# Attention products on stacked high and low halves, in a ring of two head pairs

## The reference

```python
n = rms_norm(h, norm1_g[layer]);  proj = n @ w_in[layer]
mq = rms_norm(mq, moba_q_norm_g);  mk = rms_norm(mk, moba_k_norm_g)
p = softmax(mq @ mk.T * 64**-0.5 + t5_bias[bucket(distance)], causal)
y_moba = p @ mv
```

```python
c = cumsum(log_sigmoid(x @ w_f + b_f))
p = softmax(q @ k.T * 64**-0.5 + c[query] - c[key], causal)
y_fox = p @ v
```

## Time and profile before

| what | value |
|---|---|
| runs | 2238.19 us median, 2237.45 to 2238.38 |
| the profiled execution | 2238.22 us, of which the span is 2236.3 |
| outside the span | 1.9 us |
| PE busy | 2166.0 us, 97% of the span |
| DVE / ACT / POOL busy | 1072.5 / 840.2 / 124.7 us |
| mean granted TensorE clock | 0.986 |

### The profile page before, as it was taken

The page is one execution under the profiler, slowest core; times in us unless marked ns, Lnnn a source line. Parts: engine busy times, 40 slices in busy tenths (PEclk is TensorE's granted clock), DMA queues, the critical chain, the costliest instruction groups (busy, mean ns, idle before and its releaser), DMA issues.

```text
span 2236.3 us, 23914 instructions
## 1 busy us (share of the span) xinstructions
PE 2166.0 (97%) x9656; PEld 1691.4 (76%) x9656; DVE 1072.5 (48%) x1677; ACT 840.2 (38%) x1333; POOL 124.7 (6%) x121
## 2 busy tenths in 40 slices
PE   7999999999999999999998999998999998999997
PEld 5766767888888888766677888887766677888886
DVE  4443454655443444355466333337455466333336
ACT  4333232524332323333456243343433345342343
POOL 0000000000000000022001000002022002000001
PEclk9999999999999999999998999999999998999998
DMA  6211212422222322321222322231322221322221
GB/s 226 75 57 57 63 58 68 132 94 95 94 95 94 110 89 85 118 81 61 71 76 63 107 94 94 95 96 55 119 72 69 71 76 57 112 96 94 95 94 57
DMA packets 178794, 196.65 MB, mean 88 GB/s; under 512 B 6587, under 2 KB 164539, under 8 KB 178684
## 3 DMA queue, kind: packets, MB, share of 16 engines
q1 hardware_dynamic: 177120, 189.97, 26.6%
q0 software_dynamic: 1056, 4.72, 0.6%
q10 hardware_dynamic: 508, 0.43, 0.1%
HBM read 190.36 MB, written 4.75 MB: 87 GB/s over the span
## 4 chain that ended last, share of the span: by engine, by line
PE 90%; DVE 6%; ACT 3%; issue 1%; DMA 0%; ACTq 0%; DVEq 0%
PE ps L251 24%; PE ps L254 24%; PE ps L253 24%; PE ps L524 3%; PE ps L561 2%; PE ps L319 2%; PE ps L324 2%; PE ps L322 2%; PE ps L547 1%; PE ps L1291 1%; ACT H L1005 1%; PE ps L1277 1%; DVE wl L224 1%; ACT Phi L1008 1%; DVE d L952 1%
## 5 line engine op out<-in xcount | busy, mean ns | idle before, releaser
L251 PE MATMUL ps<-Phi,wh 128*128 128x512 f32 (+1 forms) x1520 | 614.3, 404 | 34.5 <-DVE Plo L1009 20.6
L254 PE MATMUL ps<-Phi,wl 128*128 128x512 f32 (+1 forms) x1520 | 588.7, 387 | 0.0
L253 PE MATMUL ps<-Plo,wh 128*128 128x512 f32 (+1 forms) x1520 | 588.4, 387 | 0.0
L224 DVE TENSOR_TENSOR wl<-stage,wh 128x1024 fp32r<-128x1024 f32 x333 | 406.3, 1222 | 160.2 <-ACT wh L223 145.4
L223 ACT ACTIVATE wh<-stage 128x1024 fp32r<-128x1024 f32 (+2 forms) x339 | 351.4, 1043 | 290.9 <-PE ps L254 278.4
L251 PE MATMUL ps<-Qhi,wh 128*128 128x512 f32 (+1 forms) x1056 | 402.1, 381 | 0.8 <-DVE Qlo L374 0.8
L253 PE MATMUL ps<-Qlo,wh 128*128 128x512 f32 (+1 forms) x1056 | 398.3, 377 | 0.0
L254 PE MATMUL ps<-Qhi,wl 128*128 128x512 f32 (+1 forms) x1056 | 398.3, 377 | 0.0
L251 PEld LDWEIGHTS ps<-Phi,wh 128*128 128x128 f32 x1520 | 291.9, 192 | 108.3 <-issue 47.6
L254 PEld LDWEIGHTS ps<-Phi,wl 128*128 128x128 f32 x1520 | 291.2, 192 | 57.6
L253 PEld LDWEIGHTS ps<-Plo,wh 128*128 128x128 f32 x1520 | 292.2, 192 | 54.5 <-issue 4.6
(11 more groups left out here) (245 smaller groups left out, 1725.0 us busy)
## 6 DMA issues: line engine op xcount, KB each, us to landing
stage<-in_w_ff SPq DMA_DIRECT2D x64, 1024.0 KB, 5.2
stage<-in_w_in SPq DMA_DIRECT2D x54, 1024.0 KB, 5.3
stage<-in_w_up SPq DMA_DIRECT2D x16, 1024.0 KB, 5.3
stage<-in_w_down SPq DMA_DIRECT2D x16, 1024.0 KB, 5.1
stage<-in_w_out SPq DMA_DIRECT2D x12, 1024.0 KB, 5.1
stage<-in_w_bg SPq DMA_DIRECT2D x4, 1024.0 KB, 5.3
x_Cb<-cneg SPq DMA_DIRECT2D x16, 256.0 KB, 5.6
vrev<-rev POOLq DMA_DIRECT2D x1, 2560.0 KB, 9.1
```

Source lines behind the costliest of these rows:

```text
L224: t_lo = low.op(lambda e: e.tensor_tensor(lo, src, hi.bitcast(F32), ALU.subtract), st_landed[n], t_hi, w_free[i % 4], sem=s_wlo if low is ...
L251: PE.op(lambda e: e.matmul(o, hi[:, k, c], x.hi[:, kx, tok], start=first, stop=False), t_hi, t_x or x.t[kx], list(waits), signal=False)
L253: PE.op(lambda e: e.matmul(o, hi[:, k, c], x.lo[:, kx, tok], start=False, stop=False), signal=False)
L254: return PE.op(lambda e: e.matmul(o, lo[:, k, c], x.hi[:, kx, tok], start=False, stop=last), t_lo, sem=s_wpe, signal=last)
```

## The change

What it does, part by part:

- The scores are float32r. A tile `qs` per head holds the high part of q on 64 partitions and its low part on the other 64; `kh` holds the high part of k on both halves, `kl` its low part on both. Two matmuls over 128 partitions, `qs` by `kh` and `qs` by `kl`, give all four products. The second copy of `kh` and `kl` is made by DMAs from POOL's queue (four for each pair of heads).
- The values are stored per head as 64 high and 64 low columns (`split_values`). The transposed probabilities are split too: ACT writes the high part, a new DVE subtraction the low part (`turn`). `weigh` is eight float32r matmuls with 128 output rows, of which `both_halves` (ACT copy, DVE addition) adds the upper and the lower 64, for every head.
- The multiplication of `normalise` moves from DVE to ACT. All three attentions have four `pS` buffers, and `weigh` waits for the next head's first block.
- The mask of Fox is added by POOL to the bias (one `tensor_tensor` of 128 columns per block) in place of the bf16 matmul.
- q and k live in a ring of two head pairs. Their GEMM columns are taken pair by pair: pair 0, the values, then pairs 1 to 3 among the other columns; the attention starts after the values. A pair's weights are two pieces of 128 columns, loaded by two DMAs. `qk_norm` comes three ticks after a tile's evacuation. The paces are 0.42 and 0.53. The GLA gate columns (`gemm_thin`) move behind the attention, and MoBA's bias is loaded head by head.
- In the Fox layers the ring, the buffers and the bias take the room of `H`, which SP writes to DRAM at the start of the layer (`t_park`) and reads back after the attention (`t_back`). Many buffers have new addresses, left out below.

```diff
             for j, c in enumerate(cuts):
-                pieces.append((n, c, j == len(cuts) - 1))
+                pieces.append((n, 0, c, j == len(cuts) - 1))
+
+        def pair_cols(src, j):
+
+            v = src.rearrange("(k p) c -> p k c", p=128)
+            n = len(slabs)
+            slabs.append([(v[:, :, c:c + 128], 8, 128, o) for o, c in ((0, 128 * j), (1024, 512 + 128 * j))])
+            pieces.append((n, 0, (0, 8, 0, 128), False))
+            pieces.append((n, 1, (0, 8, 0, 128), True))
...
-            dst = stage[n % 2][:, 0:nk * ncol].rearrange("p (k c) -> p k c", k=nk)
-            st_landed[n] = SP.op(lambda e: e.dma_start(dst, v), st_free[n % 2], sem=s_st[n % 2], inc=16)
+            for v, nk, ncol, o in slabs[n]:
+                dst = stage[n % 2][:, o:o + nk * ncol].rearrange("p (k c) -> p k c", k=nk)
...
+            def ready(self, h):
+                return h > 7 or len(self.t.get(h, ())) == 2
+
...
+                ts = []
+                for h in (2 * j, 2 * j + 1):
+                    qs, r, other = self.tiles(h)[0], hp(h), hp(h + 1)
+                    hi, x = qs[r, :], src[r, :]
+                    t1 = A.op(lambda e, hi=hi, x=x: e.activation(hi, x, ACT.Copy, scale=sc), t, wait)
+                    t2 = V.op(lambda e, hi=hi, x=x, qs=qs, other=other: e.scalar_tensor_tensor(
+                        out=qs[other, :], in0=x, scalar=sc, in1=hi.bitcast(F32), op0=ALU.mult, op1=ALU.subtract), t1, t)
+                    self.t.setdefault(h, []).append([t1, t2])
+                    ts += [t1, t2]
+                return ts
+
+            def keys(self, j, src, t, *waits):
+
+                wait = [self.room(j), list(waits)]
+                ts = []
+                for h in (2 * j, 2 * j + 1):
+                    _, kh, kl = self.tiles(h)
+                    r, other, s = hp(h), hp(h + 1), s_dup[j % 2][h % 2]
+                    hi, lo, x = kh[r, :], kl[r, :], src[r, :]
+                    t1 = A.op(lambda e, hi=hi, x=x: e.activation(hi, x, ACT.Copy), t, wait)
+                    t2 = V.op(lambda e, hi=hi, lo=lo, x=x: e.tensor_tensor(lo, x, hi.bitcast(F32), ALU.subtract), t1, t)
+                    G.op(lambda e, hi=hi, kh=kh, other=other: e.dma_start(kh[other, :], hi), t1, wait, sem=s, inc=16)
+                    t3 = G.op(lambda e, lo=lo, kl=kl, other=other: e.dma_start(kl[other, :], lo), t2, wait, sem=s, inc=16)
+                    self.t.setdefault(h, []).append([t1, t2, t3])
+                    ts += [t1, t2]
+                return ts
+
+        val_free = [None, None]
+
+        def qk_norm(heads, m, t_in):
+
+            j, v, s = m // 2, val[m % 2], sq[m % 2]
+            t = A.op(lambda e: e.activation(s[:, :], v[:, :], ACT.Square), t_in, sq_free[m % 2])
             t = PE.op(lambda e: e.matmul(banks[7][:, :], blk, s[:, :], start=True, stop=True), t, free[7], t_const)
-            sq_free[j % 2] = t
             t = A.op(lambda e: e.activation(tB[:, :], banks[7][:, :], ACT.Ln, bias=epsc), t, rb_free[0])
...
-            t_qk[j] = t
-
-        pS_free, PT_free = [None] * 4, [None, None]
-        t_mv = [None] * 4
-
-        def softmax_heads(q_of, k_of, v_of, t_q, t_k, t_v, bias_of, masked, finished):
+            sq_free[m % 2] = t
+            if m % 2:
+                val_free[1] = heads.keys(j, v, t, t_xread)
+            else:
+                val_free[0] = heads.queries(j, v, t, 1.0, t_xread)
+
+        def softmax_heads(heads, vv, t_v, bias_of, finished):
 
             t_exp, t_pt, t_norm, biases = {}, {}, {}, {}
+            hi_T, lo_T = PT
 
             def bias_for(n):
                 if n < 32:
...
+                if n % 8 == 7:
+                    heads.last_score[n // 8] = t
                 t = V.op(lambda e: e.tensor_tensor_reduce(p[:, 0:w], banks[sb][:, 0:w], bias, -1.0, 3.0e38,
                                                           ALU.add, ALU.min, nm[:, c:c + 1]), t, t_b, pS_free[n % len(pS)])
-                free[sb] = bias_read[n % 2] = t
+                free[sb] = bias_read[n % 2] = bias_done[n] = t
                 t_exp[n] = A.op(lambda e: e.activation(p[:, 0:w], p[:, 0:w], ACT.Exp, bias=nm[:, c:c + 1], scale=-1.0,
                                                        accum_out=sm[:, c:c + 1]), t)
 
@@ -537,33 +629,33 @@
...
+                t_norm[n] = A.op(lambda e: e.activation(p[:, 0:w], p[:, 0:w], ACT.Copy, scale=ri[:, c:c + 1]), t)
 
...
                 for j in range(i + 1):
                     t2 = PE.op(lambda e, j=j: e.transpose(banks[6][:, 128 * j:128 * j + 128],
                                                           p[:, 128 * j:128 * j + 128], ident), t, free[6])
                 pS_free[n % len(pS)] = t2
-                t = A.op(lambda e: e.activation(pt[:, 0:i + 1, 128 * i:128 * i + 128],
-                                                banks[6][:, 0:w].rearrange("p (j q) -> p j q", j=i + 1), ACT.Copy),
-                         t2, PT_free[pn])
-                free[6] = t
-                t_pt.setdefault(h, []).append(t)
+                hi, lo = (x[:, i:4 * i + 1:3, :] for x in (hi_T, lo_T))
+                src = banks[6][:, 0:w].rearrange("p (j q) -> p j q", j=i + 1)
+                t = A.op(lambda e: e.activation(hi, src, ACT.Copy), t2, PT_free[0])
+                t2 = V.op(lambda e: e.tensor_tensor(lo, src, hi.bitcast(F32), ALU.subtract), t, t2)
+                free[6] = [t, t2]
+                t_pt.setdefault(h, []).append([t, t2])
 
             def weigh(h):
-                pt, pn = PT[h % len(PT)], h % len(PT)
-                o = banks[7][64 * (h % 2):64 * (h % 2) + 64, :]
+                o = banks[7][:, :]
                 for j in range(4):
-                    v = v_of(h, j)
-                    t = PE.op(lambda e, j=j, v=v: e.matmul(o[:, 128 * j:S], v, pt[:, j, 128 * j:S],
-                                                           start=(j == 0), stop=(j == 3)),
-                              t_pt[h], t_v, free[7] if h % 2 == 0 else None)
-                PT_free[pn] = t
-                if h % 2:
-                    free[7] = finished(h // 2, banks[7][:, :], t)
+                    for x in (hi_T, lo_T):
+                        last = j == 3 and x is lo_T
...
+                while not heads.ready((n + ahead) // 4):
+                    yield
                 normalise(n + depth - 1)
                 scores(n + ahead)
                 bias_for(n + ahead + 2)
-                if n >= 4 and n % 4 == 0 and len(PT) > 1:
+                yield
+                if n >= 4 and n % 4 == 0:
                     weigh(n // 4 - 1)
-                yield
                 turn(n)
                 yield
-                if n % 4 == 3 and len(PT) == 1:
-                    yield
-                    weigh(n // 4)
-            if len(PT) > 1:
-                weigh(7)
+            yield
+            weigh(7)
+
+        def split_values(vv, b, o, t, sc, *waits):
+
+            o8 = o.rearrange("p (h d) -> p h d", h=8)
+            hi, lo = vv[:, b, :, 0:64], vv[:, b, :, 64:128]
+            t1 = A.op(lambda e: e.activation(hi, o8, ACT.Copy, scale=sc), t, list(waits))
+            t2 = V.op(lambda e: e.scalar_tensor_tensor(out=lo, in0=o8, scalar=sc, in1=hi.bitcast(F32),
+                                                       op0=ALU.mult, op1=ALU.subtract), t1, t)
+            return [t1, t2]
+
+        def both_halves(dst, o, t, *waits):
+
+            t1 = A.op(lambda e: e.activation(dst, o[64:128, :], ACT.Copy), t, list(waits))
...
+        def ev_val(m):
             def ev(o, t):
-                t_qk[j] = to_sb(qk[:, j, :], t_rB)(o, t)
-                return t_qk[j]
+                t1 = V.op(lambda e: e.tensor_tensor(val[m % 2][:, :], o, rB[:, :], ALU.mult),
+                          t, t_rB, t_xread, val_free[m % 2])
+                after_ticks(3, lambda: qk_norm(moba, m, t1))
+                return t1
...
-        gemm_pair(P, ev_qk(0), ev_qk(1), between=first_scale)
...
+        gemm_pair(P, ev_val(0), ev_val(1), between=first_scale)
...
         gemm_tok(P, ev_mv)
-        finish_background()
...
-        pace[0] = 0.53
-        t = gemm_thin(P, glow[:, :], None)
-        t_glow.append(V.op(lambda e: e.tensor_tensor(glow[:, :], glow[:, :], rB[0:16, :], ALU.mult), t, t_rB))
+        pace[0] = 0.42
...
+        for ev in (ev_val(2), ev_val(3), ev_gqk(0), ev_gqk(1), ev_val(4), ev_val(5), ev_gqk(2), ev_gqk(3),
+                   ev_gqk(4), ev_val(6), ev_val(7), ev_gqk(5), ev_gqk(6), ev_gqk(7)):
             gemm(P, 8, ev)
...
         finish_background()
+        t = gemm_thin(P, glow[:, :], None)
+        t_glow.append(V.op(lambda e: e.tensor_tensor(glow[:, :], glow[:, :], rB[0:16, :], ALU.mult), t, t_rB))
...
+            t_park = SP.op(lambda e: e.dma_start(parked, H[:, :, :]), t_h, sem=s_l[4], inc=16)
...
-            for j in range(2, 8):
-                gemm(P, 8, ev_fqk(j))
...
-                t_fv[b] = V.op(lambda e: e.tensor_copy(fv[:, b, :], o), t, t_ph)
```

(21 more changed lines are left out.)

248 lines of the change are left out of this document (136 added, 112 removed).

## The result

The changed kernel takes 2220.27 us (median of 4 runs, 2217.6 to 2222.7), beside 2238.28 for the kernel before in the same runs: ratio 0.992 [0.9902, 0.9937]. That is 18 us faster, not 52, and outside the range. The profiled execution took 2221.2 us, its span 2219.4, 16.9 less than before.

The account below looks back on a forecast made before the run. PE's instructions one after another were taken to bound the kernel, softmax hidden behind GEMM matmuls. PE's gain of 84 us less 32 us of waits made 52 us less than 2238.2: forecast 2186 us, range 2160 to 2212.

Parts of the forecast that it names:

- PE's gain, 84 us: PE in all three attentions: float32 scores, `weigh` and Fox mask matmuls, 146.0 us, go; float32r ones, 61.9 us, come.
- R1: Rival, 18%: narrow float32r matmuls are dear; 128 columns at 0.2 us give 2194 us, at 0.41 give 2214.
- (a): MoBA's first pair: PE waits 4.3 us between norm sums, lower clock costs 2.4; 6.7 us, bounds 4 and 12.
- (b): MoBA's six other norms: PE waits when weight pieces or softmax stand ahead; 0.7 us each, 4 us, bounds 0 and 14.
- (c): Second copy of the keys, all three attentions: chain and DMA landing nearly covered; 3 us of waits, bounds 0 and 12.
- (d): Start of each Fox attention: bias and mask come late for the first scores; 2 us a layer, 4 us, bounds 0 and 12.
- (f): Head's first weights 1 us, GLA's gate columns 1 us, retention's decay tables 1 us a layer; 4 us, bounds 0 and 12.
- (e): Attention blocks: transposes and `weigh` wait a little for ACT and DVE; 0.1 us a block, 96 blocks, 10 us, bounds 0 and 48.
- R3: Rival, 10%: DVE bounds Fox's rotary stretch, low parts reach `weigh` late; 0.3 us a block, 19 us more, 2205 us.
- R4: Rival, 5%, slower: the scores-to-transpose chain over DVE and ACT is uncovered, PE waits at each transpose; 0.9 us a block gives 2262.

Follow-up runs that it names:

- the deferral with the second bank: Against changed kernel with norms spread and reciprocal early: low parts of blocks 0-2 and halves' addition behind next scores, odd blocks' transposes in bank 7; 2195.3 us.

## Why the prediction was wrong

- **PE's gain, 84 us: right.** Pairs of 128 columns put off the next matmul by 0.23 us for 0.24; the rest is as forecast. R1 fell. Counted in the same way, the float32 forms had taken 6.06 us a head in MoBA and 6.34 in Fox, so the gain is rather 88.
- **(a), 6.7 us: right.** The gap is 4.2 us, and PE works 4.9 us at half clock behind it, 2.4 us lost.
- **(b), 4 us: mis-sized.** Five of the six later norm sums wait 3.4, 0.6, 3.2, 1.6 and 1.5 us, 10.2 in all, inside the bound of 14. Behind the two long ones the granted clock is 0.51 (75.8 to 79.2 us) and 0.50 (120.2 to 127.0), by an estimate some 5 us more. Spreading the norms gave back 5.5.
- **(c) and (d), 7 us: too high.** No wait of PE is for the second copy of the keys (128 KB landed in 2.4 to 4.4 us), and PE is busy 35.00 of 35 us from 895 to 930. This hid a part of what the other terms lack. **(f)** is near: the first GEMM matmul comes 1.0 us later (12.6 for 11.6), PE waits 0.9 for the gate columns, and GLA takes 2.7 longer, of which 1.7 is a granted clock of 0.50 from 246.5 to 249.9. The 1.0 us of the head came from no row when it was forecast.
- **(e) failed, in Fox.** "I take 0.1 us a block, 96 blocks: 10 us" was the step. In MoBA it held: PE's waits at L639 and L654 are 2.5 us for 32 blocks, and the low part costs 0.12 a block. In Fox PE is idle 32 us more than before, and the low part alone costs 26.5 us, 0.41 a block; over all blocks it is 31 us, inside the bound of 48 but outside the value taken. I added up DVE's work against the time of a GEMM (6.9 of 7.5 us) and found cover, and counted the low part as 0.28 to 0.69 us. An instruction that reads what another engine has just written also costs the engine that wait: in order, everything behind it stands too. That was 75 us on top of 47 of work. A quarter of these 122 us reached PE. The rivals had pieces of it: R3 the size (0.3 us a block) but by work in five GEMMs, where the waits run through all of Fox; R4 the uncovered chain, but from one block's bare 2.5 us, without two engines queueing for each other.
- **The multiplication** was booked as relief of DVE. It was (21 us, of which some 13 are clock), but it also made ACT wait for the reciprocal: the early reciprocal gave 7 us.
- Of 84 us of gain 66 were lost, where the forecast had 32. Removed singly, the low part (31), the norms (5.5), the mask (5) and the reciprocal's place (7) give back 49. How they add was tested only for norms with reciprocal (14 us together, 13 singly) and for the deferral with the second bank (11 more). MoBA's 26 us are 14.4 of waits at L585, 2.5 of waits in the softmax, 2 of the head and the gate columns, 5.5 of clock, and some 2 that stay open. In Fox 11 us of idle time stay without the low part, for 3 in the kernel before; their causes stay open.

## What to carry to other kernels

Where an added instruction reads another engine's fresh result, price it as work plus the time its engine stands there, with everything queued behind; busy shares of 60% on two engines that feed each other are no cover. Read what DVE and ACT wait for: waiting for PE is slack, waiting for each other is lockstep. The remedy that worked was to issue such an instruction behind the next independent one, unless its reader comes next. When such an order is changed, read PE's idle time and its granted clock apart: two of the runs here lost more by the clock than by waits.
